# Twelve slots instead of eight in the ring of gathered expert rows, and the forget mask on the query side

## The chip, the cores and the metric

The kernel runs on one core of a Trainium2 chip. The core has five engines that run their own instruction streams: PE (TensorE, matrix products), DVE (VectorE, elementwise work and reductions), ACT (ScalarE, activation functions and copies), POOL (GpSimd, which here does nothing but issue transfers) and SP (SyncE, which issues the weight transfers). They meet through semaphores. The time is device microseconds (us) for one execution; of several runs the median is given.

## What is computed

The reference runs two blocks on 256 tokens of width 1024. The first (compressed, selected and windowed attention, a linear recurrence, an MLP) is over before the change matters. The second has two layers, each a token mixer followed by a PEER feed-forward: every token looks up 8 x 16 = 128 expert rows `u` and 128 rows `v` out of 16,384 of each, every row 1024 floats:

```python
act = jax.nn.gelu(jnp.einsum('cd,ced->ce', xc, u[ec]))
return jnp.einsum('ce,ced->cd', gc.astype(xc.dtype) * act, v[ec])
```

The mixer of layer 1 is the forgetting attention of 16 heads, whose score gets the difference of two cumulative sums of log forget gates:

```python
s = jnp.einsum('bthd,bshd->bhts', qb, k).astype(jnp.float32) * scale
s = s + cq[..., :, None] - cum[..., None, :]
p = jax.nn.softmax(jnp.where(causal, s, NEG_INF), axis=-1).astype(v.dtype)
```

## The kernel before

**Tiles.** The 256 tokens are two tiles of 128. The PEER of one (layer, tile) pair is called a PEER tile here; there are four, numbered t = 0 to 3: (layer 0, tile 0), (0, 1), (1, 0), (1, 1). One expert row for each of the 128 tokens of a tile is one gather: an indirect transfer of 128 x 1024 floats (512 KB) into one slot of the ring `W` (8 slots, `GRING`). A PEER tile takes 256 gathers, 128 of `u` and 128 of `v`; `PLACE` sets their order (24 `u`, then `v` and `u` in turn, then 24 `v`).

**Who issues and who consumes.** POOL issues all 1024 gathers in that order (line 414). Gather n waits until the row n - 8, the last one in its slot, has been consumed. A `u` row is consumed on DVE (line 908: times the token's vector, summed along the row). Odd `v` rows are added to the accumulator `acc` on DVE (line 843), even ones are added on PE by two 128x512 products with a diagonal matrix that ACT makes (line 423, `psL<-W,con`). `FREED` says for each row which engine frees it.

**The order of the work.** PEER tile t is not worked off in one piece: its rows are consumed beside the next tile's mixer and search. In the programs of DVE, PE and ACT stand calls `rows(n)`, each of which consumes n rounds of 8 rows (32 rounds per PEER tile). For t = 0, 1 and 2 the calls are: one round beside each of the 8 attention steps, one before units 0 and 4 of the output projection (`residual`), one before the norm, some beside the query projection `pq..a` (two for t = 0, 1 and 2 each: `rows(before)` on DVE), and 11 to 14 in the search for the top experts (`search`, `between`); beside `oin` (the 25-unit input projection of the forget attention) there are six. What is left is done by `rows_end`. The rows of t = 3 have nothing beside them: all 32 rounds stand in the last `rows_end`. The indices of the next PEER tile (`idx_ready`) are there before POOL comes to them, except at the very start.

**Weights.** SP loads units of 512 KB into `wring` (8 slots), each as soon as PE has used the unit eight before it (`unit_done`). They run on the same 16 DMA engines as the gathers.

**The forget attention.** `lrow[r, 0:P]` holds, on two groups of partitions, 8 F[t] and -1 for each head; row `OF` of `Z` holds 1 and 8 F[s]. For each head the second product of a score adds F[t] - F[s]. Since 16 heads share the partitions, one of the two operands must be zero outside its head. Before, it is the key side: 16 products with `C("ind", 1, P, h)` per tile write `FK`, which lies in `aring`, the four-slot buffer (16 KB per partition) through which POOL loaded the `ada` weights during the first block, up to 512 us.

Of the kernel before, what the change touches and what calls it, by code (L numbers as in the profile page):

```python
# [19 lines left out]
ALU = mybir.AluOpType  # L20
AX = mybir.AxisListType

P = 128
S = 256
# [2 lines left out]
KC = D // P  # L27
WRING = 8
ARING = 4
GRING = 8  # L30
NEG = -1e30
EPS = 1e-6
NCMP = 15
# [47 lines left out]
LEAD = 24  # L81
CHUNK = 16
PER = 2 * SLOTS
NROUND = PER // GRING
PLACE = []
for _p in range(PER):
    _q = _p - LEAD
# [26 lines left out]
def build(nc, x_dram, c_row, ada, weights, small, vecs, cons, experts_u, experts_v, out):  # L114
    ctx = ExitStack()
    with ctx:
        def sb(name, shape, dt=F32):
            return ctx.enter_context(nc.sbuf_tensor(name, shape, dt))
# [19 lines left out]
        mod = sb("mod", [P, 96])  # L138
        crow = sb("crow", [P, D])

        aring = sb("aring", [P, ARING, D])
        amul = sb("amul", [P, 4 * KC])
        rstd = sb("rstd", [P, 2 * S])
        var = sb("var", [P, 2 * S])
# [30 lines left out]
        def C(name, w, parts=P, a=0):  # L175
            return con[0:parts, CON[name] + a:CON[name] + a + w]
# [14 lines left out]


        bias0, bias1 = bias[:, 0:12 * P], bias[:, 12 * P:]
        FK = aring[:].rearrange("p a d -> p (a d)")
        h_t = [Z[:, (29 + 4 * T) * S:(33 + 4 * T) * S] for T in range(NT)]
        acc = [Z[:, (37 + 4 * T) * S:(41 + 4 * T) * S] for T in range(NT)]

# [223 lines left out]
        def _(pe):  # L421
            def mm(o, l, r, first=True, last=True):
                return pe.matmul(o, l, r, start=first, stop=last)  # L423
# [6 lines left out]
            def rows(n):  # L430

                t = stream["tile"]
                if t is None:
                    return
                for r in range(stream["done"], min(stream["done"] + n, NROUND)):
                    for p in range(r * GRING, (r + 1) * GRING):
                        kind, i = PLACE[p]
                        who, count = FREED[t * PER + p]
                        if who != "pe":
                            continue  # L440
                        slot = p % GRING
                        first, last = count % V_PE == 1, count % V_PE == 0
                        if first and t:
                            pe.wait_ge(acc_taken, t)
                        pe.wait_ge(diag_ready, count)
                        pe.wait_ge(row_landed[slot], ((t * PER + p) // GRING + 1) * 16)
                        for b in range(2):
                            m = mm(pacc[:, b, :], diag[(count - 1) % 4],
                                   W[:, slot * D + b * 512:slot * D + (b + 1) * 512], first, last)
                        m.then_inc(row_pe, 1)  # L450
                    stream["done"] = r + 1
# [54 lines left out]
            def attention(kind):  # L506
                js = JOBS[kind]
                if kind in ("even1", "odd0", "odd1"):

                    pe.wait_ge(key_taken, {"even1": 4, "odd0": 8, "odd1": 12}[kind])  # L510

                def scores(jb):
                    n, T = jb["n"], jb["T"]
                    if n >= 2:
                        pe.wait_ge(smax_ready, n - 1)
                    w = keys_of(T)
                    for m in range(2):
                        r = jb["rows"][m]

                        o = (psL if m else psS)[:, n % 2, 0:w]  # L520
                        last = mm(o, toks(Z, jb["q"][m], T, r), toks(Z, jb["k"][m], 0, r, w),
                                  True, jb["kind"] != "forget")
                        if jb["kind"] == "forget":
                            h = jb["head"][m]
                            last = mm(o, lrow[r, 0:P], FK[r, h * S:h * S + w], False, True)
                    last.then_inc(scores_ready, 1)

                def turn_maps(jb):
                    n, T = jb["n"], jb["T"]
                    pe.wait_ge(p_ready, n + 1)  # L530
                    if n >= 1:
                        pe.wait_ge(pt_copied, n)
                    at = 0
                    for m in range(2):
                        for kt in range(T + 1):
                            last = pe.transpose(psT[:, at * P:(at + 1) * P],  # L536
                                                Pb[:, n % 2, m * S + kt * P:m * S + (kt + 1) * P], ident)
                            at += 1
                    last.then_inc(pt_ready, 1)

                def values(jb):
                    n, T = jb["n"], jb["T"]
                    pe.wait_ge(pt_copied, n + 1)
                    if n >= 1:
                        pe.wait_ge(o_copied, n)
                    for slot in sorted(set(jb["slot"])):
                        parts = [(m, kt) for m in range(2) if jb["slot"][m] == slot for kt in range(T + 1)]
                        o = psO[:, slot * P:(slot + 1) * P]
                        for a, (m, kt) in enumerate(parts):
                            at = m * (T + 1) + kt  # L550
                            last = mm(o, jb["v"][m](kt), PT[:, n % 2, at * P:(at + 1) * P], a == 0,
                                      a == len(parts) - 1 and jb["cmp"] is None)
                        if jb["cmp"] is not None:
                            c = jb["cmp"]
                            last = mm(o, VTc[0:NCMP, 0:P], W[0:NCMP, 6144 + c * P:6144 + (c + 1) * P],
                                      False, True)
                    last.then_inc(o_ready, 1)

                scores(js[0])
                scores(js[1])  # L560
                for a, jb in enumerate(js):
                    turn_maps(jb)
                    if a + 2 < len(js):
                        scores(js[a + 2])
                    if kind == "nsa":
                        for u in in2_beside(a):
                            in2_unit(u)
                    values(jb)
                    rows(1)
# [263 lines left out]
        def _(dve):  # L833
# [50 lines left out]
            def rows(n):  # L884
# [4 lines left out]
                    return  # L889
                T = t % NT  # L890
                for r in range(stream["done"], min(stream["done"] + n, NROUND)):
                    for p in range(r * GRING, (r + 1) * GRING):
                        kind, i = PLACE[p]
                        who, count = FREED[t * PER + p]
                        slot, col = p % GRING, T * SLOTS + i
                        row = W[:, slot * D:(slot + 1) * D]
                        if kind == "v" and i % CHUNK == 0:

# [474 lines left out]
            def odd(T):  # L1373
# [27 lines left out]
                    m = dve.memset(f[q:q + 32, :], 1.0)  # L1401
                link(m)
                for h in range(16):
                    m = ts(FK[:, h * S + T * P:h * S + (T + 1) * P], f, C("ind", 1, P, h), None, ALU.mult)
                m.then_inc(f_ready, 1)
                attention(f"odd{T}")
                residual(f"oout{T}", 48 + 16, T)
# [14 lines left out]
        def _(act):  # L1422
# [20 lines left out]
            def rows(n):  # L1443
# [2 lines left out]
                if t is None:  # L1446
                    return
                for r in range(stream["done"], min(stream["done"] + n, NROUND)):
                    for p in range(r * GRING, (r + 1) * GRING):
                        kind, i = PLACE[p]  # L1450
                        who, count = FREED[t * PER + p]
                        col = t % NT * SLOTS + i
# [335 lines left out]
```

## Time and profile before

| | us |
|---|---|
| median of three runs (2661.26 to 2667.13) | 2664.3 |
| the profiled execution, whole | 2653.54 |
| its span, first to last instruction | 2651.9 |
| gathers: first issued at | 864.93 |

| engine | busy us | share of the span |
|---|---|---|
| PE | 1790.7 | 68% |
| DVE | 1618.2 | 61% |
| POOL | 1212.9 | 46% |
| ACT | 370.0 | 14% |

Shares are averages over the whole span. The change acts in the stretch in which gathers run, from 865 us to the end, so its rows are read from there. A wait is listed under the engine that waited and the one whose event came last. "issue" for POOL is time between two gathers in which it waited for nothing that the profile shows.

### The profile page before, as it was taken

To read this page: it belongs to the slowest core of one execution; us is meant where nothing else is said; L and a number is where in the kernel's file an instruction comes from. 1 tells how busy PE (TensorE), PEld (TensorE's weight loads), DVE (VectorE), ACT (ScalarE), POOL (GpSimd) and SP (SyncE) were. 2 spreads that over 40 slices of the span, in tenths; PEclk is the share of its full clock that TensorE was granted. 3 is DMA by queue.
4 is the path that set the end of the run, shared out by engine and by line. 5 is a ranking of instruction groups with operands and counts; after the bars stand their busy time and mean duration, and the time that the engine had idled before them with its cause. 6 is when DMAs were issued, how large, how long until landed. Compare 5 with 4: busy or idle time off the path is not lost.

```text
span 2651.9 us, 23297 instructions
## 1 busy us (share of the span) xinstructions
PE 1790.7 (68%) x7234; PEld 1217.1 (46%) x7234; DVE 1618.2 (61%) x3441; ACT 370.0 (14%) x977; POOL 1212.9 (46%) x1124
## 2 busy tenths in 40 slices
PE   7999689998968056665556666556566765255565
PEld 6887578886847034431145244225443632011112
DVE  3348425402154986688665756886476598667764
ACT  1012401000121021100112211011121110000001
POOL 1001001100000476467764775676467467777774
PEclk9899899998969568886878878877878877667768
DMA  9547348842415489999998898999979988899996
GB/s 322 186 161 232 121 129 326 308 154 98 135 40 191 152 308 338 350 371 328 358 365 352 319 352 332 341 340 350 383 259 342 349 317 318 313 374 397 396 374 250
DMA packets 210157, 757.92 MB, mean 286 GB/s; under 512 B 23036, under 2 KB 26248, under 8 KB 209800
## 3 DMA queue, kind: packets, MB, share of 16 engines
q0 software_dynamic: 161280, 587.27, 60.2%
q1 hardware_dynamic: 48344, 167.35, 18.0%
q10 hardware_dynamic: 432, 2.03, 0.2%
q8 instruction: 53, 0.87, 0.1%
q14 instruction: 48, 0.39, 0.0%
HBM read 755.50 MB, written 1.07 MB: 285 GB/s over the span
## 4 chain that ended last, share of the span: by engine, by line
PE 36%; POOL 21%; DMA 17%; DVE 16%; issue 8%; ACT 2%; POOLq 0%; DVEq 0%; ACTq 0%
PE psL L423 30%; POOL W L414 21%; DMA W<-experts_v,crow 15%; PE psS L423 3%; PE psO L423 2%; DVE W L908 2%; DVE Z L843 1%; DMA W<-experts_u,crow 1%; DVE N L843 1%; DVE bias L1313 1%; DVE Z L849 1%; PE psT L536 1%; DVE bias L1316 1%; DVE Sb L843 1%; ACT W L1432 1%
## 5 line engine op out<-in xcount | busy, mean ns | idle before, releaser
L423 PE MATMUL psL<-W,con 128*128 128x512 f32 x1024 | 666.2, 793 | 502.5 <-DMA W<-experts_v,crow 359.4
L414 POOL DMA_INDIRECT W<-experts_u,crow x512 | 602.7, 1177 | 672.5 <-DVE crow L846 358.8
L908 DVE SCALAR_TENSOR_TENSOR W<-W,Z 128x1024 f32<-128x1024 f32 x512 | 618.8, 1225 | 326.8 <-DMA W<-experts_u,crow 323.7
L414 POOL DMA_INDIRECT W<-experts_v,crow x512 | 559.2, 1092 | 283.2 <-PE psL L423 140.7
L423 PE MATMUL psL<-N,wring 128*128 128x256 f32 (+1 forms) x3568 | 627.4, 339 | 74.8 <-DVE N L846 60.7
L423 PEld LDWEIGHTS psL<-W,con 128*128 128x128 f32 x1024 | 227.2, 242 | 888.0 <-issue 732.7
L423 PEld LDWEIGHTS psL<-N,wring 128*128 128x128 f32 x3568 | 566.0, 201 | 147.3 <-DVE N L846 65.0
L843 DVE SCALAR_TENSOR_TENSOR Z<-W,crow,Z 128x1024 f32<-128x1024 f32 x252 | 323.6, 1284 | 104.7 <-DMA W<-experts_v,crow 100.7
L398 POOL DMA_DIRECT2D aring<-ada x96 | 50.9, 530 | 454.7 <-DVE aring L1038 453.8
L1432 ACT ACTIVATE Z<-psL 128x128 f32<-128x128 f32 (+2 forms) x190 | 60.4, 319 | 627.6 <-PE psL L423 627.6
L536 PE MATMUL psT<-con,Pb 128*128 128x128 f32 x144 | 34.6, 364 | 162.9 <-DVE Pb L846 162.9
L1432 ACT ACTIVATE con<-con,crow 128x128 f32<-128x128 f32 x256 | 86.0, 390 | 392.0 <-DVE crow L849 374.2
L1038 DVE SCALAR_TENSOR_TENSOR aring<-aring,crow 128x1024 f32<-128x1024 f32 x96 | 115.3, 1219 | 8.5 <-DMA aring<-ada 8.2
L423 PE MATMUL psL<-Z,wring 128*128 128x256 f32 x528 | 115.7, 383 | 1.5 <-DVE Z L849 1.5
L423 PEld LDWEIGHTS psL<-Z,wring 128*128 128x128 f32 x528 | 101.4, 192 | 15.7 <-ACT Z L1432 1.9
L536 PEld LDWEIGHTS psT<-con,Pb 128*128 128x128 f32 x144 | 19.6, 176 | 187.9 <-DVE Pb L846 186.7
L423 PE MATMUL psL<-AT,wring 128*128 128x128 f32 (+1 forms) x576 | 82.3, 309 | 30.2 <-DVE N L849 18.7
L423 PEld LDWEIGHTS psL<-AT,wring 128*128 128x128 f32 x576 | 79.2, 212 | 39.1 <-issue 29.0
L849 DVE TENSOR_TENSOR X<-psL,X 128x256 f32<-128x256 f32 x16 | 6.8, 425 | 131.0 <-PE psL L423 131.0
L1432 ACT ACT_TABLE_LOAD x54 | 69.3, 1283 | 12.2 <-DMA crow<-c_row 11.3
L1432 ACT ACTIVATE Pb<-Sb,mx 128x128 f32<-128x128 f32 (+1 forms) x96 | 42.7, 446 | 188.5 <-DVE mx L846 188.4
L1432 ACT ACTIVATE crow<-crow 128x16 f32<-128x16 f32 (+2 forms) x43 | 11.0, 257 | 405.4 <-DVE W L908 344.4
(197 smaller groups left out, 1371.8 us busy)
## 6 DMA issues: line engine op xcount, KB each, us to landing
wring<-weights SPq DMA_DIRECT2D x311, 512.0 KB, 4.8
aring<-ada POOLq DMA_DIRECT2D x96, 512.0 KB, 5.8
W<-experts_u,crow POOLq DMA_INDIRECT x512, 6.3
W<-experts_v,crow POOLq DMA_INDIRECT x512, 6.2
W<-rel_rows SPq DMA_DIRECT2D x1, 1536.0 KB, 9.0
X<-x_dram ACTq DMA_DIRECT2D x1, 1024.0 KB, 6.0
out<-N SPq DMA_DIRECT2D x1, 1024.0 KB, 3.9
W<-rel_rows SPq DMA_DIRECT2D x1, 768.0 KB, 4.9
```

The lines of the kernel that those rows point to most:

```text
L398: pool.dma_start(aring[:, j, :], src).then_inc(ada_landed[j], 16)
L414: pool.indirect_dma_start(W[:, slot * D:(slot + 1) * D], None, experts_u if kind == "u" else experts_v, bass.IndirectOffsetOnAxis(ap=idx[: ...
L423: return pe.matmul(o, l, r, start=first, stop=last)
L536: last = pe.transpose(psT[:, at * P:(at + 1) * P], Pb[:, n % 2, m * S + kt * P:m * S + (kt + 1) * P], ident)
L843: return dve.scalar_tensor_tensor(out=o, in0=a, scalar=s, in1=b, op0=op0, op1=op1)
L849: return dve.tensor_tensor(o, a, b, op)
L908: dve.scalar_tensor_tensor(out=row, in0=row, scalar=1.0, in1=h_t[T], op0=ALU.mult, op1=ALU.mult, accum_out=dots[:, col:col + 1]).then_inc( ...
L1038: dve.scalar_tensor_tensor(out=aring[:, slot, :], in0=aring[:, slot, :], scalar=1.0, in1=crow[:], op0=ALU.mult, op1=ALU.mult, accum_out=mo ...
L1313: dve.max_index(out=ix[:, a, 0:8], in_max=v[:, a, 0:8], in_values=src[:, a, :])
L1316: m = dve.match_replace(out=src[:, a, :], in_to_replace=v[:, a, 0:8], in_values=src[:, a, :], imm_value=-3e38)
L1432: return act.activation(o, i, fn, **k)
```

## The change

Three edits.

1. `GRING` becomes 12, and the size of a round, which was the same number, becomes a constant of its own, `ROUND = 8`. Gather n now waits for row n - 12. The slot of a row is `(t * PER + p) % GRING`, since 256 is no multiple of 12. `W` grows by four slots.
2. The buffer `aring` is gone. The `ada` weights go through slots 8 to 11 of `W`. The memory used is the same.
3. `FK` is gone with it. The 16 products per tile now mask `row` (`lrow`), the query side, and write into `N`; the second product of a score takes `N[r, h * P:(h + 1) * P]` and the unmasked row `OF` of `Z`.

```diff
-GRING = 8
+GRING = 12
+ROUND = 8
...
-NROUND = PER // GRING
+NROUND = PER // ROUND
...
-        aring = sb("aring", [P, ARING, D])
...
-        FK = aring[:].rearrange("p a d -> p (a d)")
+        aring = W[:, 8 * D:(8 + ARING) * D].rearrange("p (a d) -> p a d", a=ARING)
...
-                    for p in range(r * GRING, (r + 1) * GRING):
+                    for p in range(r * ROUND, (r + 1) * ROUND):
...
-                        slot = p % GRING
+                        slot = (t * PER + p) % GRING
...
-                            last = mm(o, lrow[r, 0:P], FK[r, h * S:h * S + w], False, True)
+                            last = mm(o, N[r, h * P:(h + 1) * P], toks(Z, OF, 0, r, w), False, True)
...
-                    m = ts(FK[:, h * S + T * P:h * S + (T + 1) * P], f, C("ind", 1, P, h), None, ALU.mult)
+                    m = ts(N[:, h * P:(h + 1) * P], row, C("ind", 1, P, h), None, ALU.mult)
```

No engine gets an instruction more or less, and none changes its place. What differs is which row a wait names. On POOL, at the first gathers of PEER tile 0, `row_dve` counts the rows that DVE has consumed. Before:

```order
L414 DMA W<-experts_u,crow 128x1024 [waits idx_ready]
L414 DMA W<-experts_u,crow 128x1024 x7
L414 DMA W<-experts_u,crow 128x1024 [waits row_dve] x17
L414 DMA W<-experts_v,crow 128x1024 [waits row_dve]
L414 DMA W<-experts_u,crow 128x1024 [waits row_dve]
```

After:

```order
L414 DMA W<-experts_u,crow 128x1024 [waits idx_ready]
L414 DMA W<-experts_u,crow 128x1024 x11
L414 DMA W<-experts_u,crow 128x1024 [waits row_dve] x13
L414 DMA W<-experts_v,crow 128x1024 [waits row_dve]
L414 DMA W<-experts_u,crow 128x1024 [waits row_dve]
```

Twelve gathers instead of eight go out before the first one that waits for a consumed row, and every later one waits for a row four earlier.

On PE, in an attention step of the even layer, `psT` takes the turned probabilities, `psS` and `psL` the scores, `psO` the values, and `psL<-W,con` are the `v` rows. Before:

```order
L423 MATMUL psO<-PT,VT 128x128 x3
L423 MATMUL psL<-W,con 128x512 [waits row_landed1,diag_ready]
L423 MATMUL psL<-W,con 128x512
L423 MATMUL psL<-W,con 128x512 [waits row_landed5,diag_ready]
L423 MATMUL psL<-W,con 128x512
L536 MATMUL psT<-con,Pb 128x128 [waits pt_copied,p_ready]
```

After:

```order
L423 MATMUL psO<-PT,VT 128x128 x3
L423 MATMUL psL<-W,con 128x512 [waits row_landed9,diag_ready]
L423 MATMUL psL<-W,con 128x512
L423 MATMUL psL<-W,con 128x512 [waits row_landed1,diag_ready]
L423 MATMUL psL<-W,con 128x512
L536 MATMUL psT<-con,Pb 128x128 [waits pt_copied,p_ready]
```

The same two rows stand at the same place; only their slots differ.

## Rows read from the trace of the kernel before

**Rows 1.** Page, part 4: shares of the chain that ended last, by line.

```profile
PE psL L423 30%; POOL W L414 21%; DMA W<-experts_v,crow 15%; PE psS L423 3%; PE psO L423 2%; DVE W L908 2%; DVE Z L843 1%; DMA W<-experts_u,crow 1%; DVE N L843 1%; DVE bias L1313 1%; DVE Z L849 1%; PE psT L536 1%; DVE bias L1316 1%; DVE Sb L843 1%; ACT W L1432 1%
```

**Rows 2.** Page, part 5: busy us, mean ns of one, idle before with its cause.

```profile
L414 POOL DMA_INDIRECT W<-experts_u,crow x512 | 602.7, 1177 | 672.5 <-DVE crow L846 358.8
L908 DVE SCALAR_TENSOR_TENSOR W<-W,Z 128x1024 f32<-128x1024 f32 x512 | 618.8, 1225 | 326.8 <-DMA W<-experts_u,crow 323.7
L414 POOL DMA_INDIRECT W<-experts_v,crow x512 | 559.2, 1092 | 283.2 <-PE psL L423 140.7
```

**Rows 3.** Waits of POOL over the span: us in total, times, longest us.

```profile
POOL W L414 <- issue: 275.2, 892, 3.3
POOL W L414 <- DVE W L908: 179.8, 53, 20.8
POOL W L414 <- PE psL L423: 142.0, 78, 9.8
```

**Rows 4.** Windows: length, then PE, PEld, DVE, ACT, POOL busy, PE clock, DMA share, GB/s.

```profile
865.00:2630.00 1765.00, 1027.20 (x3610) 568.55 (x3610) 1265.39 (x2546) 225.98 (x621) 1161.81 (x1024) 0.76 0.91 339
...
1335.00:1440.00 105.00, 71.51 (x456) 58.70 (x456) 62.42 (x109) 15.28 (x48) 60.59 (x52) 0.80 0.99 382
...
2440.00:2460.00 20.00, 11.74 (x16) 3.71 (x16) 14.93 (x20) 1.28 (x4) 14.69 (x16) 0.76 1.03 410
```

**Rows 5.** Timeline of POOL: start, duration, gather, idle before and its cause.

```profile
895.40 1.68 POOL L414 DMA_INDIRECT W<-experts_u,crow  x1 [20.76 <-DVE W L908]
```

**Rows 6.** Waits, 942 to 1027 us, the first attention with rows beside it.

```profile
DVE W L908 <- DMA W<-experts_u,crow: 15.4, 12, 2.9
...
POOL W L414 <- PE psL L423: 7.1, 2, 4.1
```

**Rows 7.** Waits of DVE, 1027 to 1072 us, the output projection behind it.

```profile
DVE W L908 <- DMA W<-experts_u,crow: 5.4, 3, 2.8
```

**Rows 8.** Timeline around the query projection `pq01a` of PEER tile 1.

```profile
1085.57 0.94 POOL L414 DMA_INDIRECT W<-experts_v,crow  x1 [9.44 <-PE psL L423]
...
1091.93 1.23 DVE L908 SCALAR_TENSOR_TENSOR W<-W,Z 128x1024 f32<-128x1024 f32 x1 [10.76 <-DMA W<-experts_u,crow]
...
1100.48 2.72 PE L423 MATMUL psL<-W,con 128*128 128x512 f32 x4 [3.68 <-DMA W<-experts_v,crow]
...
1105.01 0.60 ACT L1432 ACTIVATE bias<-psS 128x512 f32<-128x512 f32 x1 [9.96 <-PE psS L423]
```

**Rows 9.** Windows: the first forget attention, and the gap ahead of the second.

```profile
1440.00:1572.00 132.00, 77.41 (x248) 40.60 (x248) 91.40 (x200) 27.18 (x74) 94.91 (x77) 0.74 0.85 307
...
1920.00:1940.00 20.00, 13.99 (x54) 9.28 (x56) 17.28 (x46) 5.07 (x17) 4.71 (x4) 0.64 0.20 61
```

**Rows 10.** Timeline of POOL at the start of the two forget attentions.

```profile
1456.33 1.89 POOL L414 DMA_INDIRECT W<-experts_u,crow  x1 [11.15 <-DVE W L908]
...
1930.41 1.89 POOL L414 DMA_INDIRECT W<-experts_u,crow  x1 [14.89 <-DVE W L908]
```

**Rows 11.** Waits of DVE and POOL, 1639 to 1804 us, the second search.

```profile
DVE Z L843 <- DMA W<-experts_v,crow: 12.5, 7, 3.0
DVE W L908 <- DMA W<-experts_u,crow: 7.4, 7, 2.4
...
POOL W L414 <- DVE W L908: 21.5, 8, 8.2
POOL W L414 <- PE psL L423: 6.0, 4, 2.4
```

**Rows 12.** Page, part 6: size of a transfer, median us from issue to landing.

```profile
wring<-weights SPq DMA_DIRECT2D x311, 512.0 KB, 4.8
...
W<-experts_u,crow POOLq DMA_INDIRECT x512, 6.3
```

**Rows 13.** Waits of POOL, 2274 to 2630 us, the rows of PEER tile 3.

```profile
POOL W L414 <- PE psL L423: 10.1, 19, 2.0
```

**Rows 14.** Instructions on `aring`: the head mask of the forget attention.

```profile
L846 DVE TENSOR_SCALAR aring<-Z,con x32: 276/281/286, 1447.6 to 1922.3; 128x128 f32<-128x128 f32 x32
```

More of the change, by code:

```diff
@@ L891, in rows @@
                 for r in range(stream["done"], min(stream["done"] + n, NROUND)):
-                    for p in range(r * GRING, (r + 1) * GRING):
+                    for p in range(r * ROUND, (r + 1) * ROUND):
                         kind, i = PLACE[p]
                         who, count = FREED[t * PER + p]
-                        slot, col = p % GRING, T * SLOTS + i
+                        slot, col = (t * PER + p) % GRING, T * SLOTS + i
                         row = W[:, slot * D:(slot + 1) * D]
@@ L1448, in rows @@
                 for r in range(stream["done"], min(stream["done"] + n, NROUND)):
-                    for p in range(r * GRING, (r + 1) * GRING):
+                    for p in range(r * ROUND, (r + 1) * ROUND):
                         kind, i = PLACE[p]
```

## The prediction

> **What bounds the kernel now.** The chain that ended last comes first: more than a third of it is the gathers, as POOL's issue (21%) and as transfers of `v` rows on their way (15%), the rest of its top the products on PE [rows 1]. So the next view is of the stretch with gathers, 865 to 2630 us. In its 1765 us POOL is busy 1161.8, DVE 1265.4, PE 1027.2, and the DMA engines carry 339 GB/s at a share of 0.91, where a stretch of nothing but gathers shows 410 at 1.03 [rows 4]. Nobody is full. The waits say why: a ring of eight lets work change hands in turns. POOL stands 179.8 us for a slot that DVE must free and 142.0 for one that PE must free, 322 together [rows 3]; DVE in turn stands 323.7 us for `u` rows that have not landed [rows 2]. POOL's own time is what remains when the slots are free: 602.7 + 559.2 busy and 275.2 between gathers, 1437 us for 1024 gathers, 1.40 us each [rows 2, 3]. Those 1437 stay whatever the ring.
>
> So there are two kinds of stretches. Where DVE has much other work, the ring is full and POOL stands; where it has little, DVE runs on POOL's heels and POOL sets the pace. Four more slots carry four gathers from the first kind into the second. One such head start is worth 4 x 1.40 = **5.6 us**, if POOL stood that long before and if DVE (or PE) waits for rows after.
>
> **The change part by part.**
>
> *The mask.* Before and after, 16 products of 128x128 per tile, 281 ns each in the median [rows 14], and the same score products on PE with operands of the same shape. Their input is `lrow` instead of `OF`, their output `N` instead of `FK`, and `N` has been read to the end by the projection that DVE has waited for. Cost 0. Should the other operands cost, its bound is a tenth of 32 x 0.281 us, under 1 us. The `ada` loads only change their address: 0.
>
> *The ring.* It adds no instruction. Going through the stretch:
>
> (a) First attention with rows. Ahead of it the ring is full and POOL stands 20.76 us [rows 5], so the whole head start is there. In the attention DVE waits 15.4 us for `u` rows, while POOL stands 7.1 us for slots that PE frees late [rows 6]. I take 5.6 and about a quarter of the 7.1: **7.5** (0 to 15.4).
>
> (b) Output projections, three of them. In the first DVE waits 5.4 us [rows 7]. In the second and third DVE comes from a stretch in which it ran on POOL's heels, so part of the wait stays. I take 3 each: **9** (0 to 16).
>
> (c) Query projections `pq..a`, three. Here PE holds the ring: POOL stands 9.44 us for a `v` row that PE uses only after unit 3, and the gather that PE needs after unit 7 goes out behind it, so PE stands 3.68 us for it, and the scores on which the search depends reach ACT that much later; DVE stands 10.76 meanwhile [rows 8]. With twelve slots the late row is asked for four rows earlier. What then comes last is the projection itself, which the ring doesn't move. Hence not the 10.76, but the 3.68 and a little: 4 each, **12** (0 to 32).
>
> (d) Input projections `oin`, two. POOL stands here too, but the DMA engines show a share of 0.99 and 382 GB/s [rows 4], weights included. More slots can't make full engines faster. Only what POOL stands at the edge counts: 2 each, **4** (0 to 11).
>
> (e) Forget attentions, two. Ahead of each POOL stands 11.15 and 14.89 us, and around the second the transfers fall to 61 GB/s [rows 9, 10]. In the window of the first POOL has 94.9 us of work for 77 gathers, and 77 x 0.3 us between them is 23; with the 11.15 that is 129 of the 132 us: but for the stand POOL is busy from end to end [rows 9, 10]. So it sets the pace and the head start counts whole: 2 x 5.6, **11** (5 to 15).
>
> (f) Searches, three. DVE waits 12.5 + 7.4 = 19.9 us for rows and POOL stands 27.5 for slots [rows 11], in turn, a few us each. Since the stands are shorter than 5.6 us on average (27.5 over 12 times), twelve slots could take nearly all of them; but POOL's 1.40 us a gather is close to DVE's pace there, so the ring may not fill again between two of them. I take a third of the 19.9, 7 each: **21** (0 to 50).
>
> (g) The last 32 rounds. POOL stands only 10.1 us in 356 [rows 13], the rest is issue. Only what it is ahead on entry counts: **3** (0 to 5.6).
>
> The sum is 7.5 + 9 + 12 + 4 + 11 + 21 + 3 = 67.5 us, a fifth of the 322 that POOL stands. The profiled execution took 2653.5 us, so 2586 by its own clock. The median of the runs shown is 10.8 above the profiled one; put on top, it gives **2596 us**.
>
> **The rivals.**
>
> *A smaller gain, the stand turns into something else.* A gather isn't always as long: 0.92 us in the full-rate window (14.69 / 16 [rows 4]), 1.23 in the first forget attention (94.91 / 77 [rows 9]). If gathers get longer where POOL no longer stands, (a), (b) and (f) go, and 4 + 11 + 12 + 3, with a DMA queue that lands rows a little later, leave about 25 us: 2639. For it speaks that the DMA share is 0.91 already, against it that the short gathers stand where the engines carry most, so a full queue doesn't lengthen them.
>
> *A larger gain.* All waits of DVE outside the last 32 rounds that have a stand of POOL ahead: (a) 15, (b) 16, (c) 15, (d) 6, (e) 11, (f) 45, (g) 3, 111 us: 2553. For it speaks that DVE and POOL would both have room (1265 and 1437 of 1654 us). By the Trainium skill ("DMA: Bandwidth & Descriptors", section Bandwidth) the memory gives one core some 358 GB/s and so binds transfers to SBUF; by that figure the stretch would be at least 339 x 1765 / 358 = 1671 us by estimate, which would cap the gain at 94 and rule this rival out. The trace disagrees: a window shows 410 GB/s [rows 4].
>
> *No change.* The ring is deeper but no more rows get ahead, because something else than slots holds back what is in flight. The rows show eight gathers out and never more, so they don't exclude it: 2664.
>
> *Slower: gathers crowd out the weights.* Both use the same engines. If a weight unit lands behind four more gathers, it comes 4 x 512 KB / 410 GB/s = 5.1 us later (from rows 4), and if PE stands for that once in each of the 11 projections that run beside rows (`eout1`, `oin` and `oout` twice, `pq` a and b three times), the kernel is 56 us slower: 2720. The point from which it decides is the lead of `wring`: 8 units ahead, at 105 us for 25 units of `oin` 34 us, against 4.8 us from issue to landing [rows 4, 12]. A unit would have to land seven times as late. The Trainium skill (the same page, section Queues, rings and completion order) says that a DMA engine goes round robin between the queues it has work for, packet by packet. By that rule a longer gather queue takes no more than half; half of 410 GB/s is a unit each 2.6 us by estimate, and `oin` asks for one each 4.2. No row here shows the share of each queue while both are full.
>
> **How the numbers follow.** The forecast, 45 to 95 us gained, gets 0.56; the smaller gain (7 to 45 us) 0.18; the larger 0.12; no change within 0.2%, which is about what a measurement of this kernel can tell from none, 0.07; slower 0.07. The predicted time is the forecast's, 2596. The range goes from 2550, which takes in most of the larger gain, to 2650, which takes in most of the smaller; outside are no change, slower and the outermost parts of the two, some 0.2. Faster by more than 0.2%: 0.56 + 0.18 + 0.12 = 0.86.
>
> **What would show it.** In the profile after: POOL's waits for slots fall from 322 to about 250 us while its 1437 us of own time stay; the two stands of 11 and 15 us at the forget attentions become 6 and 9; the 3.68 us of PE in `pq..a` vanish and the scores come some 4 us after the projection less; the last 32 rounds take as long as now (from 2274 to 2630 us, 356); the mask instructions still take 281 ns. If gathers average over 1.2 us instead of 1.13, the smaller gain is right. If PE waits for `wring` appear beside `oin` or `pq`, the slower rival is. The forecast is wrong if DVE's waits for rows fall but its waits for PE or ACT grow by as much in attention or search.

## The result, and the profile after

| | before | after |
|---|---|---|
| median, us | 2664.3 (2661.26 to 2667.13) | 2591.75 (2587.35 to 2596.81) |
| ratio to before | 1 | 0.9737, 95% interval 0.9714 to 0.976 |

The difference of the medians is 72.6 us, and the change is worth 2.6%. In a second measurement of the same kernel, in the first batch of experiments, the ratio was 0.9755 (0.9713 to 0.9797). One of the first five runs of the changed kernel, the profiled one, was disturbed (3557 us) and is not in the ratio, so the profile after is that of the second measurement: its span is 2599.6 us, against 2651.9 before.

First the waits of POOL over the span (us in total, times, longest), which answer to [rows 3]:

```profile
POOL W L414 <- issue: 303.6, 962, 3.1
POOL W L414 <- DVE W L908: 120.9, 20, 14.9
POOL W L414 <- PE psL L423: 113.2, 36, 9.1
POOL W L414 <- remote: 14.6, 5, 5.4
```

"Remote" is a release whose origin the trace doesn't show. The trace of before has none, and this asks for care with every cause named from the trace after. The packed trace after holds 19,486 records of semaphore updates, that of before 26,673, though the two programs have the same instructions. Up to the first gather the counts agree (5960 and 5957); behind it records are missing. The page shows it too: it gives no time from issue to landing for a gather, where before it gave 6.3 us [rows 12]. So the lengths of waits can be compared, but a wait whose release was not recorded may stand under "remote", under "issue" or under an earlier event.

Then the costliest groups of POOL and DVE (busy us, mean ns | idle before), which answer to [rows 2]:

```profile
L414 POOL DMA_INDIRECT W<-experts_u,crow x512 | 587.5, 1147 | 635.1 <-DVE crow L846 357.8
L908 DVE SCALAR_TENSOR_TENSOR W<-W,Z 128x1024 f32<-128x1024 f32 x512 | 614.6, 1224 | 226.5 <-DMA W<-experts_u,crow 198.1
L414 POOL DMA_INDIRECT W<-experts_v,crow x512 | 568.7, 1111 | 275.0 <-issue 149.8
```

POOL's stands for slots fell from 321.8 to 248.7 us, the 14.6 with an unnamed releaser among them. Its own time is 587.5 + 568.7 + 303.6 = 1460 us by these rows, 1437 before; the "issue" in it may hold stands whose release was not recorded. A gather takes 1.13 us in the mean, as before. DVE's waits for `u` rows that are put down to transfers fell by 125.6 us, from 323.7 to 198.1, and those for `v` rows by 30.2, from 100.7 to 70.5. All idle time ahead of these instructions, whatever its cause, fell by less: by 100.3 us for `u` (326.8 to 226.5) and by 21.7 for `v`, here before and after:

```profile
L843 DVE SCALAR_TENSOR_TENSOR Z<-W,crow,Z 128x1024 f32<-128x1024 f32 x252 | 323.6, 1284 | 104.7 <-DMA W<-experts_v,crow 100.7
...
L843 DVE SCALAR_TENSOR_TENSOR Z<-W,crow,Z 128x1024 f32<-128x1024 f32 x252 | 324.1, 1286 | 83.0 <-DMA W<-experts_v,crow 70.5
```

So DVE is idle 122 us less ahead of rows, and the two traces are only 52 us apart: more than half turned into other waits. Some of them, in the trace after:

```profile
ACT Z L1432 <- remote: 59.4, 13, 7.1
DVE X L843 <- remote: 41.9, 8, 11.1
DVE Z L849 <- remote: 11.3, 2, 8.8
```

The window over the stretch with gathers answers to [rows 4]. It is 57 us shorter, but it ends 4 us ahead of DVE's last row (2577.5 us); from the first gather to the end of that row the stretch is 50 us shorter (1764.4 us before, 1714.3 after).

```profile
865.00:2573.00 1708.00, 1004.98 (x3604) 564.73 (x3605) 1252.77 (x2533) 224.57 (x621) 1154.69 (x1023) 0.76 0.93 349
```

The head mask, [rows 14], now writes into `N`. Its duration (min/median/max ns) is the same:

```profile
L846 DVE TENSOR_SCALAR N<-crow,con x32: 278/279/287, 1421.2 to 1873.7; 128x128 f32<-128x128 f32 x32
```

### The profile page after: what moved, and what is told of

It reads as the page before. It is cut to its first block, busy times and chain, and to the rows that moved or that the text cites. A ratio compares the mean times of both kernels' runs of the same rounds, so it can differ in the third digit from the quotient of the medians.

```text
span 3555.7 us, 23297 instructions
## 1 busy us (share of the span) xinstructions
PE 3073.7 (86%) x7234; PEld 1879.8 (53%) x7234; DVE 1612.3 (45%) x3441; ACT 370.5 (10%) x977; POOL 1214.6 (34%) x1124
## 4 chain that ended last, share of the span: by engine, by line
PE 72%; POOL 10%; DVE 9%; issue 6%; ACT 2%; DMA 1%; another core or an unknown queue 0%; ACTq 0%; DVEq 0%
PE psL L423 64%; POOL W L414 10%; PE psO L423 3%; PE psS L423 3%; DVE W L908 2%; PE psT L536 1%; DVE Z L843 1%; DVE N L843 1%; PE psT L578 1%; DMA W<-experts_v,crow 1%; DVE N L846 0%; DVE var L955 0%; ACT con L1432 0%; DVE Z L849 0%; DVE X L843 0%
## 5 line engine op out<-in xcount | busy, mean ns | idle before, releaser
L423 PE MATMUL psL<-N,wring 128*128 128x256 f32 (+1 forms) x3568 | 1255.0, 559 | 54.7 <-DVE N L846 38.5
L423 PE MATMUL psL<-W,con 128*128 128x512 f32 x1024 | 984.2, 1152 | 228.2 <-ACT con L1432 103.9
L423 PEld LDWEIGHTS psL<-N,wring 128*128 128x128 f32 x3568 | 955.7, 329 | 367.3 <-issue 299.5
L423 PEld LDWEIGHTS psL<-W,con 128*128 128x128 f32 x1024 | 295.3, 303 | 822.8 <-issue 710.3
L423 PE MATMUL psL<-Z,wring 128*128 128x256 f32 x528 | 247.0, 678 | 1.5 <-DVE Z L849 1.5
L423 PE MATMUL psL<-AT,wring 128*128 128x128 f32 (+1 forms) x576 | 151.3, 469 | 22.6 <-DVE N L849 12.3
L423 PEld LDWEIGHTS psL<-AT,wring 128*128 128x128 f32 x576 | 139.9, 348 | 42.8 <-issue 34.6
L1038 DVE SCALAR_TENSOR_TENSOR W<-W,crow 128x1024 f32<-128x1024 f32 x96 | 114.4, 1218 | 0.2
L423 PE MATMUL psL<-W,wring 128*128 128x256 f32 (+1 forms) x224 | 89.9, 598 | 0.6 <-issue 0.6
L423 PE MATMUL psO<-PT,VT 128*128 128x128 f32 x288 | 78.7, 457 | 4.6 <-ACT PT L1432 3.3
```

The source lines that it names most:

```text
L1038: dve.scalar_tensor_tensor(out=aring[:, slot, :], in0=aring[:, slot, :], scalar=1.0, in1=crow[:], op0=ALU.mult, op1=ALU.mult, accum_out=mo ...
```

## The experiments

Three batches of four kernels, each batch on a chip of its own and beside its own runs of the kernel before. Ratios are to those runs. The medians of before were 2670.41, 2660.82 and 2651.63 us.

### The depth of the ring

One number each in the changed kernel; `W` keeps its twelve slots in memory.

```diff
-GRING = 12
+GRING = 10
...
-        W = sb("W", [P, GRING * D])
+        W = sb("W", [P, 12 * D])
```

> The changed kernel once more, for its times and an undisturbed trace. Theory (the ring's head start, place by place): 2580 to 2605 us, about 70 below the kernel before; POOL stands some 250 us for slots instead of 322, its own time stays near 1437 us (1.40 us a gather), the stands of 11 and 15 us ahead of the forget attentions fall to about 6 and 9, PE's 3.7 us in the query projection are gone. Rival (the stand turns into something else): gathers average over 1.2 us instead of 1.13.

> The change without its deeper ring: the mask on the query side and the ada weights inside W, but eight slots (W keeps the size of twelve). Theory: the mask costs and gives nothing, 2664 us, ratio to the kernel before 0.999 to 1.001. Rival (part of the gain comes from the mask or from the place of the operands): clearly below 2660 us, by as much as the ring then doesn't give.

> The changed kernel with ten slots instead of twelve. Theory (each slot is a head start of one gather, 1.4 us, at each place where POOL stood longer): half of the gain or somewhat more, since the short stands are taken first: 2617 to 2630 us. Rival (one place decides, a row that PE holds in the query projection and that needs the full four rows): little with ten, 2650 us or more.

> The changed kernel with six slots. Theory: the curve goes on and gets steeper, since a gather takes 6.3 us from issue to landing and 1.4 us to issue, so that about five are under way and six slots leave one for rows in use: 2760 us or more. Rival (slots matter only at a few long stands): the loss from eight to six is as large as the gain from eight to ten, 2700 us.

`mask_only` is `GRING = 8`, so what is left of the change is its mask side alone.

| kernel | slots | median, us | ratio, 95% interval | POOL's slot waits (DVE + PE), us |
|---|---|---|---|---|
| ring6 | 6 | 2886.4 | 1.081 (1.0773 to 1.0847) | 546.9 |
| mask_only | 8 | 2667.04 | 0.9999 (0.9977 to 1.0021) | 314.3 |
| ring10 | 10 | 2611.1 | 0.9787 (0.9756 to 0.9818) | 241.8 |
| after_again | 12 | 2604.42 | 0.9755 (0.9713 to 0.9797) | 234.1 |

The mask costs nothing and brings nothing that 0.2% could show; the whole gain is the ring's. And it flattens in this batch: by the medians 219 us from six slots to eight, 56 from eight to ten and 7 from ten to twelve, where the intervals overlap. Ten slots gave more than was expected of them, and a price per slot (1.40 us each, the same for every slot) doesn't fit. At six slots the gathers themselves are longer, too (1225 ns for `u` rows, 1163 at eight).

### Where the depth pays

The ring has twelve slots, but POOL holds a gather back as in a ring of eight unless its row is used in a chosen place of the program:

```diff
-                if n >= GRING:
-                    who, count = FREED[n - GRING]
+                held = GRING if deep(n) else 8
+                if n >= held:
+                    who, count = FREED[n - held]
```

`deep(n)` goes by the round of eight rows: attention, projections (output and `pq..a` together), search, or the rest (`oin` and the last 32 rounds).

> Twelve slots, but only the gathers for the attention rounds (rounds 0 to 8 of PEER tile 0, 7 to 14 of tiles 1 and 2) may run twelve ahead; all others wait for the row eight earlier, as before. Theory (the head start is taken where POOL stood long and DVE then runs on its heels): the attention rounds give 25 to 32 us, 2635 to 2642 with 2667 for eight slots. Rival (the prediction's sum): its terms (a) and (e), 18.5 us, 2648.

> As deep_att, but twelve ahead only for the rounds of the searches and the few behind them (14 to 31 of tile 0, 20 to 31 of tiles 1 and 2). Theory (the waits are a few us each and the ring fills again between them): 30 to 40 us, 2627 to 2637. Rival (the prediction's sum): its term (f), 21 us, 2646.

> As deep_att, but twelve ahead only for the rounds beside the output projection, the norm and the first query projection (9 to 13 of tile 0, 15 to 19 of tiles 1 and 2). Theory (here more gathers in flight slow the hand-over between PE, DVE and ACT and the weight units, as the trace of the changed kernel has it): nothing or a loss, 2664 to 2680. Rival (the prediction's terms (b) and (c), the row that PE holds): 21 us gained, 2646.

> The changed kernel with the projection rounds of deep_proj held to eight ahead, all others twelve. Theory (the projections lose about 10 us of the gain): 2580 to 2596 us, faster than the changed kernel by 5 to 15. Rival (terms (b) and (c) were gained): 2615 us, slower than the changed kernel by some 15.

| kernel | twelve slots for | ratio, 95% interval | gained, us |
|---|---|---|---|
| deep_att | attentions | 0.9911 (0.9881 to 0.994) | 24 |
| deep_search | searches | 0.992 (0.9898 to 0.9943) | 21 |
| deep_proj | output projections and `pq..a` | 0.9975 (0.9955 to 0.9995) | 7 |
| flat_proj | all but those | 0.978 (0.9756 to 0.9805) | 59 |

Attention and search each hold a third of the gain. The projections bring 7 us where the prediction had 21, and leaving them out costs almost nothing (59 of 65 to 70); nor does it make the kernel 5 to 15 us faster, as I had expected. The lengths of the stages say where the time goes. The two kernels on the left are of the first batch, the two on the right of the second. They are taken from the start of DVE's rows of a round to the start of the next stage's, and summed over the places of a kind (three each, two for `oin`; "last" is from round 4 of PEER tile 3 to its end), in us:

| stage | mask_only | after_again | flat_proj | deep_proj |
|---|---|---|---|---|
| attentions | 307.3 | 277.6 | 276.4 | 308.2 |
| output projections | 145.3 | 159.5 | 145.7 | 142.8 |
| `pq..a` | 122.7 | 118.8 | 137.1 | 108.2 |
| `oin` | 245.2 | 237.7 | 239.4 | 250.5 |
| last | 321.6 | 317.6 | 317.7 | 321.1 |
| searches | 453.5 | 417.7 | 420.2 | 451.8 |

Alone, depth shortens `pq..a` by 14.5 us. In the whole ring of twelve it shortens them by 3.9, and the output projections ahead of them grow by 14.2. Here is such a place, the second output projection in the profile after; DVE takes unit after unit:

```profile
1529.26 1.28 DVE L843 SCALAR_TENSOR_TENSOR Z<-W,crow,Z 128x1024 f32<-128x1024 f32 x1 [0.16 <-DMA W<-experts_v,crow]
...
1531.28 0.35 DVE L843 SCALAR_TENSOR_TENSOR X<-psL,mod,X 128x128 f32<-128x128 f32 x1 [0.74 <-remote]
...
1531.78 2.02 PE L423 MATMUL psL<-AT,wring 128*128 128x128 f32 x16 [0.25 <-issue]
...
1542.69 0.61 DVE L843 SCALAR_TENSOR_TENSOR X<-psL,mod,X 128x128 f32<-128x128 f32 x2 [11.06 <-remote]
...
1543.19 2.05 PE L423 MATMUL psL<-AT,wring 128*128 128x128 f32 x8 [9.39 <-DVE X L843]
```

DVE waits 11.06 us for the second unit, whose products PE's records place ahead of 1531.8. It is the update of the semaphore that comes late, not DVE: the packed trace has it at 1542.67 us, 0.02 us ahead of DVE's start. In that gap gathers load the DMA engines to the full (window: ..., DMA share, GB/s):

```profile
1530.00:1543.00 13.00, 3.55 (x30) 3.19 (x28) 1.20 (x4) 0.31 (x1) 7.65 (x8) 0.75 1.00 396
```

I took this for the price of depth in the output projections, and the third batch was made to collect it.

### The third batch: holding back the output projections only

> Twelve slots everywhere, but gathers whose rows are used beside the three output projections (eout1, oout0, oout1) wait as in a ring of eight. It computes the same. Theory A (in the full ring of twelve the query projections pq..a gain and the output projections lose): against the run in which both kinds of projection were held to eight, pq..a are shorter by 5.3 + 8.3 + 4.7 = 18 us (39 to 40 us each in place of 45 to 47) and the output projections stay at 45, 49 and 51 us; the ratio to the kernel before is 0.978 less 18/2660, so 0.971 (2583 us). Rival B (what is held back in the output projections is only paid in pq..a, since the row that pq..a needs is then asked for too late): pq..a stay at 45 us and the ratio at 0.978. Rival C (the longer output projections hide work that comes later): output projections shorter, search longer, ratio 0.975 as for twelve everywhere.

> Twelve slots only for rows used beside the query projections pq..a, eight everywhere else. It computes the same. If the gain of the projections stands in pq..a alone (theory A): these three stages take 36 us each in place of 38 to 41, together some 14 us less, and the ratio is 0.995. If the head start has to be made before, in the output projections, to be of use here (rival B): the stages stay near 40 us and the ratio is 1.000. If the search gives it back (as where all projections were deep, 0.9975): pq..a shorter and search longer, ratio 0.998.

> Twelve slots only for rows used beside the input projections oin0 and oin1 and in the last 32 rounds, eight everywhere else. It computes the same. The prediction counted 4 + 3 = 7 us for them, ratio 0.9974. What is left of the run with projections held to eight (59 us) after attentions (24) and searches (21), 14 us, would be a ratio of 0.995 if the parts add up. If they don't (the rest is gained only where the ring arrives full from the attention or the search before), 1.000.

For `early12` PE and ACT do a round of rows ahead of the projection:

```diff
+                early = int(BESIDE[l, T][0] == 2)
                 for half, name in enumerate((f"pq{l}{T}a", f"pq{l}{T}b")):
+                    e = early if half == 0 else 0
+                    rows(e)
...
-                                   lambda j: spread(BESIDE[l, T][half], j, 8))
+                                   lambda j: spread(BESIDE[l, T][half] - e, j, 8))
```

> Twelve slots everywhere, as in the changed kernel, but PE and ACT do the first of the two rounds of rows of pq..a ahead of unit 0 and not after unit 3 (in the three pq..a that have two); the second stays after unit 7. It computes the same. If, with twelve slots, the late use of rows by PE still costs the query projections something, the three stages fall by 2 to 4 us each and the ratio is 0.971. If the projection's own units set the end there (what the prediction said of twelve slots), nothing changes: 0.975. If PE has to wait for the row's gate before unit 0, each stage grows by up to a round of rows, 7 us: 0.983.

| kernel | median, us | ratio, 95% interval | out. proj. | `pq..a` | searches | last |
|---|---|---|---|---|---|---|
| flat_out | 2528.46 | 0.9563 (0.9517 to 0.961) | 144.8 | 105.8 | 410.6 | 291.4 |
| early12 | 2521.8 | 0.9523 (0.9484 to 0.9561) | 138.0 | 101.6 | 410.0 | 293.6 |
| deep_rest | 2622.44 | 0.9916 (0.9881 to 0.9951) | 142.3 | 123.4 | 450.7 | 294.4 |
| deep_pq | 2641.09 | 0.9949 (0.9929 to 0.997) | 142.0 | 104.7 | 453.9 | 327.3 |

None of the expectations named 2520 us, and `deep_rest` gained 22 us where at most 14 were expected. What follows, in order of certainty:

**Depth in `pq..a` pays by itself.** On one chip, `deep_pq` against `deep_rest` (which holds them to eight): 104.7 against 123.4 us, 5.3, 7.9 and 5.5 in the three places. Against the kernel before, `deep_pq` gains 13.5 us (0.9949). Here is the second of them in `early12`: ACT takes its units each 1.79 us, and waits 4.45 us for the first scores (9.96 in the first such place before [rows 8]).

```profile
1571.51 0.28 ACT L1435 ACTIVATE Z<-psL 128x128 f32<-128x128 f32 x1 [1.51 <-PE psL L423]
1573.29 0.28 ACT L1435 ACTIVATE Z<-psL 128x128 f32<-128x128 f32 x1 [1.51 <-PE psL L423]
1575.08 0.28 ACT L1435 ACTIVATE Z<-psL 128x128 f32<-128x128 f32 x1 [1.51 <-PE psL L423]
...
1580.39 0.60 ACT L1435 ACTIVATE bias<-psS 128x512 f32<-128x512 f32 x1 [4.45 <-PE psS L423]
```

**Longer output projections are not the price of depth.** `early12` has twelve slots there too, and they take 138.0 us, less than with eight (5.7 of the 7.3 us between it and `mask_only` are in the first place). And `ring10`, of the same batch as the changed kernel, takes 144.7 us there and 114.2 for the `pq..a`: two slots less, and no loss. The DVE of `early12` takes the units of the place shown above every 1.79 us:

```profile
1518.95 0.35 DVE L846 SCALAR_TENSOR_TENSOR X<-psL,mod,X 128x128 f32<-128x128 f32 x1 [1.51 <-PE psL L423]
1520.74 0.35 DVE L846 SCALAR_TENSOR_TENSOR X<-psL,mod,X 128x128 f32<-128x128 f32 x1 [1.44 <-PE psL L423]
1522.52 0.35 DVE L846 SCALAR_TENSOR_TENSOR X<-psL,mod,X 128x128 f32<-128x128 f32 x1 [1.44 <-PE psL L423]
1524.31 0.35 DVE L846 SCALAR_TENSOR_TENSOR X<-psL,mod,X 128x128 f32<-128x128 f32 x1 [1.44 <-PE psL L423]
```

The four traces of this batch show no remote release at all. All eight of the first two batches do, `mask_only` with its eight slots among them (ACT 54.7 us). The same eight lack 6% (`ring6`, 24,960 left) to 27% (`after_again`, 19,486 left) of the semaphore records, all behind the first gather, while the four here have all 26,673, as the trace of the kernel before has. Part 6 of the page shows the difference; first `after_again`, then `early12`, which has the time to landing:

```profile
W<-experts_u,crow POOLq DMA_INDIRECT x512
...
W<-experts_u,crow POOLq DMA_INDIRECT x512, 6.5
```

So the late hand-over belongs to something in those executions which this batch did not have, and depth at most makes it dearer (DVE's part of it, on `X`: 8.0 us with eight slots, 21.2 with ten, 41.9 with twelve, 10.5 in `flat_proj`). That the recording of the executions itself has a part in it is a rival that no run here excludes. Here are the shares by engine of the chain that ended last, of `after_again` and of `early12`; a release without a record leaves more to "issue" and less to DMA, so their difference is in part one of recording:

```profile
PE 37%; POOL 23%; DVE 17%; issue 13%; DMA 5%; another core or an unknown queue 3%; ACT 2%; POOLq 0%; DVEq 0%; ACTq 0%
```

```profile
PE 37%; POOL 24%; DVE 17%; DMA 11%; issue 9%; ACT 2%; POOLq 0%; DVEq 0%; ACTq 0%
```

**The last 32 rounds gain where nothing interrupts the transfers.** The instructions of that stretch are the same in `flat_out`, `early12`, `deep_rest`, `flat_proj` and the changed kernel, all with twelve slots. It takes 291 to 294 us in the three of the third batch and 318 in the two others. With eight slots it takes 327 (`deep_pq`, third batch), 322 (`mask_only`, first) and 306 in the trace of the kernel before. So `deep_rest` is 33 us shorter there than `deep_pq`, `after_again` 4 shorter than `mask_only`, and 11 longer than before; traces with eight slots differ by 21 among themselves. The GB/s of the 164 us up to the end, in 40 slices, show how. Before (2460 to 2624 us):

```profile
GB/s 408 410 412 408 411 411 407 412 409 406 409 399 328 304 395 395 340 399 382 383 369 372 387 392 310 404 387 331 409 364 365 387 327 403 369 362 389 370 348 392
```

After, in `after_again` (2405 to 2569 us):

```profile
GB/s 348 394 332 393 341 341 404 329 411 350 377 401 389 364 387 363 328 404 336 383 383 373 396 384 402 410 413 410 410 410 411 411 225 193 306 388 371 397 385 348
```

In `flat_out` (2334 to 2498 us):

```profile
GB/s 412 406 412 411 408 412 408 411 411 408 407 413 394 410 402 414 406 410 412 408 410 413 406 411 412 407 413 408 409 413 404 413 410 410 411 409 410 408 402 30
```

There are two ways in which this stretch runs: an even one at 410 GB/s and a ragged one at 300 to 410. Before, the first 49 us of these are even, the end of some 100 us in that way, and then it turns ragged without a break. `deep_pq`, with eight slots in the third batch, never gets into the even way. In `after_again` it is there three times, each time until a break ends it; here is the one that ends the first and the one that ends the second (2245 to 2405 us, 4 us a slice):

```profile
GB/s 288 323 358 407 315 348 405 310 402 390 414 398 414 405 406 411 409 410 409 409 331 288 228 239 370 395 290 355 421 411 410 410 410 410 410 410 410 391 99 331
```

In `flat_out` and `early12` it stays even from 2254 us at the latest to the end, some 240 us. At 410 GB/s a row of 512 KB takes 1.28 us, and 224 gathers (rounds 4 to 31) 287 us: with twelve slots the DMA engines bound these rounds, and 291.4 us is close to that bound. POOL's gathers there take 0.99 us in the mean, and 1.15 in the ragged `deep_pq`.

**What stays open.** The breaks in the even way stand in a trace that has unnamed releases and lacks semaphore records, and the batch without those has no break; that they have one cause is likely, and not shown. Nor is it known that the flattening from ten slots to twelve would be there without them: ten slots did not run in the third batch. The changed kernel itself did not run in the third batch. `early12` differs from it in three stages only, which account for 17 us of the 81 between the two traces; the other 64 are in stages with the same instructions. So it is not shown how much of 0.9523 is the edit and how much the chip or its neighbours. Nor is it shown what the unnamed releases of the first two batches are, and why a unit of PE is seen 10 us late. What speaks against the chip alone is that the kernel before varies by 0.7% over the batches (2670, 2661, 2652). Whether `early12` beats `flat_out` isn't shown either: the intervals overlap. Both are 4.4% and more faster than the kernel before.

## Why the prediction was right, and where it was not

The forecast was 2596 us, the time is 2591.75. (The terms give 2664.3 - 67.5 = 2596.8.) The mechanism and the total were right; several of the terms were not, and that they made up for each other is luck. The terms against the difference of `mask_only` and `after_again`, two kernels of one batch that differ in the ring alone:

| term | predicted | stages of the two traces | one kind deep, whole kernel |
|---|---|---|---|
| (a) + (e) attentions | 18.5 | 29.7 | 24 |
| (b) output projections | 9 | -14.2 | (b) + (c): 7 |
| (c) `pq..a` | 12 | 3.9 | alone: 13.5 |
| (d) `oin` | 4 | 7.5 | (d) + (g): 22 |
| (f) searches | 21 | 35.8 | 21 |
| (g) last 32 rounds | 3 | 6.8 | |
| between a search and the next tile | 0 | -12.1 | |
| sum | 67.5 | 57.4 | |

In this table (g) is all 32 rounds; the "last" above leaves out the first four. The third column is from different batches: (b) + (c) and (f) of the second, `pq..a` alone and (d) + (g) of the third.

- **Bound and mechanism** held. Work changed hands in turns: POOL's stands fell to 248.7 us (250 predicted) in a trace that lacks releases. The full traces of the two fastest kernels with twelve slots bear the mechanism out better than the number: the stands are 183 (`early12`) and 187 us (`flat_out`), POOL's own time is 1441 and 1438 us, DVE's waits for `u` rows are 206 and 220. The mask cost nothing.
- **(a), (e), attentions: too small.** The step "one head start, four gathers, 5.6 us" takes it that a head start is used once. In an attention DVE and POOL can change places several times, and each change uses the slots again; the lengths fit this, the changes were not counted. In the first one DVE's waits for `u` rows fell from 15.4 us [rows 6] to 6.2, and in the whole attention 6.9 us were won; in the two forget attentions 10.9 and 11.9, twice the head start. That the stands of 11.15 and 14.89 us ahead of them [rows 10] would become 6 and 9 was wrong. The ring, now further ahead, fills all the same, and both stands are there in full, each followed by one of 3 us:

```profile
1429.94 1.89 POOL L414 DMA_INDIRECT W<-experts_u,crow  x1 [11.12 <-DVE W L908]
1434.90 1.63 POOL L414 DMA_INDIRECT W<-experts_v,crow  x1 [3.07 <-PE psL L423]
...
1881.79 1.89 POOL L414 DMA_INDIRECT W<-experts_u,crow  x1 [13.65 <-DVE W L908]
1886.86 1.52 POOL L414 DMA_INDIRECT W<-experts_v,crow  x1 [3.17 <-PE psL L423]
```

  A stand ahead of a stage doesn't measure what more slots are worth; the waits of the consumer inside the stage do.
- **(b), output projections: wrong in sign** in the traces at hand. The step took "part of the wait stays" as the only risk. The waits for rows did go (5.4 us in the first [rows 7], none there after the change; 3.2 are left in the second), and DVE waits for late units took their place. Where these are absent (`early12`), the three are 7.3 us shorter than in `mask_only`, 9 predicted; that comparison goes across two batches and two orders of work.
- **(c), `pq..a`: right in the place, hidden in the sum.** The 3.68 us of PE are gone in `pq01a` [rows 8]: PE's rows come without a wait for a transfer, after one for their scale, and ACT waits 6.05 us for the first scores where it was 9.96 [rows 8]: the 4 us less that the prediction named.

```profile
1086.13 5.30 PE L423 MATMUL psL<-W,con 128*128 128x512 f32 x8 [2.71 <-ACT con L1432]
...
1092.41 0.60 ACT L1432 ACTIVATE bias<-psS 128x512 f32<-128x512 f32 x1 [6.05 <-issue]
```

  But units of the same projection arrive late (ACT waits 3.60 and 4.08 us where 1.51 is the rule), and this eats the gain. It costs PE speed as well: the eight products above take 5.30 us, 3.70 elsewhere, for after 2.7 idle us of PE the granted clock from 1086 to 1089 us is 0.50, the lower of its two levels (1.2 GHz).

```profile
1086.00:1089.00 3.00, 2.87 (x4) 1.32 (x5) 0.00 (x0) 0.36 (x2) 0.00 (x0) 0.50 1.02 416
```

  The late units:

```profile
1080.98 0.28 ACT L1432 ACTIVATE Z<-psL 128x128 f32<-128x128 f32 x1 [3.60 <-PE psL L423]
1085.34 0.45 ACT L1432 ACTIVATE Z<-psL 128x128 f32<-128x128 f32 x2 [4.08 <-remote]
```

  Without that, the term is 13.5 (`deep_pq`) against 12.
- **(f), searches: 21 by itself, 36 in the whole.** Of the 19.9 us of DVE's waits for rows [rows 11], 14.2 lie in the second search itself (1647 to 1788 us) and the rest behind it; of those not a third went but nearly all. In the trace after 1.6 us are left, and the stage is 13.6 us shorter than in `mask_only`. The reason given for a third, that POOL's pace is close to DVE's and the ring doesn't fill again, was too careful. In `deep_search` the searches win 36 us too (417.7), yet the kernel wins 21, as predicted: the `pq..a` ahead of them, with eight slots, take 138.7 us there and not 122.7. Why they do is open. The boundary of the two stages is the first round of rows within the search, so (c) and (f) are best read together: 33 predicted, 39.7 found.

```profile
DVE Z L843 <- DMA W<-experts_v,crow: 1.6, 2, 1.3
```

- **(g), last rounds.** Near enough in the first two batches (318 against 322 with eight slots; from 2220 to 2578 us the whole takes 358, as long as before). The argument failed in the third: "POOL stands only 10.1 us, the rest is issue" left out that the engines there moved 370 GB/s (2274 to 2630 us, before) of the 410 that [rows 4] show, and that POOL's time has long gathers in it.
- **The rivals.** Smaller gain: the mean gather stayed at 1.13 us, under its mark of 1.2. Slower: PE shows no wait for `wring`; the output projections grow by 14 us and not by 56, and hardly by a weight behind four gathers, since `early12` has as many slots and no such wait. Larger gain (2553): not in the measured pair, but two kernels with twelve slots went below it, to 2522 and 2528. The cap of 94 us that a bandwidth would set falls with that: `early12` moves 365 GB/s over its whole stretch with gathers, and the last rounds of `flat_out` run at 404 to 414.

```profile
865.00:2500.00 1635.00, 979.10 (x3618) 549.05 (x3618) 1260.98 (x2549) 224.53 (x621) 1149.20 (x1024) 0.79 0.96 365
```

The Trainium skill ("DMA: Bandwidth & Descriptors", section Bandwidth) gives some 358 GB/s for one core's share of the memory, and the prediction took it as a bound. The same section says that this is the share when both cores of a pair stream, and lists 425 GB/s for a 16 MB transfer with the other core idle. The traces agree with the second figure: 365 over 1635 us in `early12` and 410 over some 240. For the shortest time that a stretch of gathers can take here, the measured 410 is the one to divide by.

## What to carry to other kernels

Depth between a producer and a consumer pays wherever the two change places, each time they do, so count the consumer's waits inside a stage and not the producer's stand ahead of it. How far it pays has to be measured: here 219, 56 and 7 us for two more slots each, the last step within the noise and only in a batch whose traces have late hand-overs. Before you compare waits by their cause, see that both traces have their releases; the lengths of stages and the idle time ahead of an instruction hold in any case. Divide the bytes of a stretch by the best rate that a window of the same trace shows before you call it bound by issue: 370 of 410 GB/s was a gain of up to 33 us (`deep_pq` to `deep_rest`) that no row on waits named. And when the sum comes out right, still compare its terms stage by stage; here the attentions and searches were 11 and 15 us better than counted, the output projections, `pq..a` and the gaps between tiles 23, 8 and 12 worse.

## What the runs showed of the hardware

- A train of 128-row gathers has an even and a ragged way to run, with the same instructions: 410 GB/s with gathers of 0.94 to 1.05 us on POOL, or 300 to 410 GB/s with single gathers of 1.3 to 2.0 us between them. Twelve in flight held the even way for some 240 us where no break came, eight for some 100 in one trace and never in another.
- A unit of PE was seen by DVE up to 11 us late while gathers moved 396 GB/s: the semaphore's update is recorded at 1542.67 us, the unit's products before 1531.8. Waits of this kind stand in two batches of three. The cause is open.
- Traces of one program can differ in completeness: 26,673 semaphore records or down to 19,486, all that is missing behind the first gather, and only in the executions that have the late hand-overs.
- With six slots `u` gathers were longer, 1225 ns in the mean; with eight (1163, and 1177 in the kernel before), ten (1173) and twelve (1147) they hardly differ.
